# Two decoder layers with product-key experts on one core: the gather ring is cut from eight rows to five after its first 128 slots, and the rows set free hold input weights of the second layer

## The chip, the cores and the metric

One core of one Trainium2 chip runs the whole kernel as one program. The metric is the device time of one execution in microseconds (us); the median over the runs is compared. The engines are named as in the profile: PE (TensorE) multiplies matrices, PEld is its weight load, DVE is VectorE, ACT is ScalarE, POOL is GpSimd, SP is SyncE, which here only issues transfers.

## What is computed

Two layers over 256 tokens of 1024 float32 numbers. Layer 0 mixes tokens by differential attention, layer 1 by a short gated convolution; after each comes a product-key expert layer (16384 experts, 8 heads, 16 chosen each). What matters here, cut from the reference:

```python
def short_conv(h, w_in, conv_w, w_out):                     # layer 1
    bcx = h @ w_in                                          # 1024 x 3072: six chunks of 512 columns
    b_gate, c_gate, xin = bcx[..., :D], bcx[..., D:2*D], bcx[..., 2*D:]
    ...
    return (b_gate * zc) @ w_out

def peer_ffn(h, w_q, sub_keys, u_tab, v_tab):               # after both layers
    q = (xt @ w_q).reshape(T, PEER_HEADS, 2, PEER_HALF)
    ...                                                     # top 16 of 16 x 16 pairs, for each of 8 heads
    act = jnp.einsum('chkd,cd->chk', u_tab[ib], xb)         # each token reads its own 128 rows of u
    act = (jax.nn.gelu(act.astype(F32)) * gb).astype(xb.dtype)
    return jnp.einsum('chk,chkd->cd', act, v_tab[ib])       # and its own 128 rows of v
```

## The kernel before

The 256 tokens of each layer are two halves of 128, and a half of a layer is a *window*: windows 0 and 1 are layer 0, windows 2 and 3 are layer 1. Each window has 128 *slots* (8 heads by 16 experts), 512 in all (`ALL`). In slot s every one of the 128 tokens gathers one expert, the row u and the row v together: 8 KB on each of 128 partitions, 1 MiB a slot. The slots are counted in the order of their issue.

The gathered rows go round a ring in memory, `ring`, of eight rows (`RING = 8`, `ring_at`, `slot`). What one slot does:

- POOL waits until `v_used` says that slot s - 8 has been read, and issues the gather of slot s (L737).
- DVE waits for the landing and takes the dot product with the token (L1421), in `dot`.
- ACT makes gelu, weight and a diagonal matrix of it (L960, L962, L966), in `weigh`.
- PE adds diagonal times v to the sum in two banks (L634, in `add_expert`) and raises `v_used`.

PE reads the slot's row last, so from landing to that matmul the row is occupied, and a new request for it can go out only then.

Beside the slots run *sides*: generators that hang the rest of the work (the mixing, projections, ranking) on slot numbers. `AT` gives for window n the offset at which each step begins, counted from the start of window n - 1; window 2 is prepared in slots 128 to 255, window 3 in slots 256 to 383, and slots 384 to 511 have only the last rankings beside them. A projection is eight steps of one slot each (`project`), so on PE an expert's two matmuls and one projection matmul take turns.

A projection's weights are a *chunk*: 1024 rows by 512 columns, 2 MiB, written `(n, what, c)`: window, matrix (`in`, `out`, `wq`), chunk. SP issues the chunks in the order of the list `loads` (`load_stream`, L687, for the buffer `stream`, place 0, in two halves of 1 MiB that are refilled as each has been read; L703 for the places that hold a whole chunk). Since SP works in order, a load waits for all that stand before it. Windows 2 and 3 use the same matrices. The set `SHARED` names those chunks of window 1 and 3 that are still held from the window before and are not loaded again: of layer 1 these are input chunks 2 and 3, both output chunks and query chunks 2 and 3.

Of the kernel before, what the change touches and what calls it, by code (L numbers as in the profile page):

```python
# [18 lines left out]
KT = D // P  # L19
# [8 lines left out]
SLOTS = PH * TOPK  # L28
RING = 8
# [28 lines left out]
def steady_of(n):  # L58
# [27 lines left out]
          (3, "in", 2), (3, "in", 3), (3, "out", 0), (3, "out", 1), (3, "wq", 2), (3, "wq", 3)}  # L86
# [56 lines left out]
def build(nc, consts, x_rows, x_cols, bias_rows, ffn_rows, w_qkv, w_o, conv_w_in, conv_w_out, peer_w_q, peer_keys, peer_uv, out):  # L143
    with ExitStack() as ctx:
# [95 lines left out]
        w_in = {place: sem(f"w_in{place}") for place in range(2, 10)}  # L240
# [43 lines left out]
        STREAM = 0  # L284
        places = {STREAM: stream[:, :], 6: spare[:, :], 7: kept[:, 0, :], 8: kept[:, 1, :], 9: kept_work}
# [6 lines left out]
        loads += [(2, "in", 2, 6), (2, "out", 0, 8), (2, "in", 4, STREAM), (2, "in", 3, 7), (2, "out", 1, 9), (2, "in", 5, STREAM), (2, "in", 0, STREAM),  # L292
                  (2, "in", 1, STREAM), (2, "wq", 0, STREAM), (2, "wq", 1, STREAM)]
        loads += [(3, "in", 4, STREAM), (2, "wq", 2, 6), (3, "in", 5, STREAM), (2, "wq", 3, 7), (3, "in", 0, STREAM), (3, "in", 1, STREAM),
                  (3, "wq", 0, STREAM), (3, "wq", 1, STREAM)]
        held_at = {}
        for place in places:
            for i, load in enumerate(load for load in loads if load[3] == place):
                held_at[load[:3]] = place, i

        def ring_at(s):
            return (2, 3, 6, 7, 4, 5, 0, 1)[s % RING]

        def slot(s):

            return ring[:, ring_at(s), :], uv_in[ring_at(s)], 16 * (s // RING + 1)
# [25 lines left out]
        def weights(n, what, c):  # L332

            place, before = held(n, what, c)
            return places[place].rearrange("p (k n) -> p k n", k=KT)
# [14 lines left out]
        def _(pe):  # L350
# [7 lines left out]
            def wait_weights(n, what, c, k):  # L358

                place, before = held(n, what, c)  # L360
                if place == STREAM:
                    if k % DEEP == 0:
                        pe.wait_ge(part_in[k // DEEP], 16 * (before + 1))
# [8 lines left out]
            def project_part(pool, n, what, c, src, ks, columns=slice(0, CHUNK), part=""):  # L372

                by_row = weights(n, what, c)
# [5 lines left out]
                for k in ks:  # L380
                    wait_weights(n, what, c, k)
                    mm = nc.tensor.matmul(bank[:, 0:width], src[:, k, :], by_row[:, k, columns], start=(k == 0), stop=(k == KT - 1))  # L382
                    if k == KT - 1:
                        mm.then_inc(pool.written_sem(key), 1)
                    elif k % DEEP == DEEP - 1 and held(n, what, c)[0] == STREAM:
                        mm.then_inc(part_used, 1)
# [72 lines left out]
            def front():  # L459
# [6 lines left out]
                by_row = weights(0, "in", 0)  # L466
                bank = take(pp, (0, "in", 0))
                for k in every:
# [7 lines left out]
                    mm = nc.tensor.matmul(bank[:, :], xT[:, k, :], by_row[:, k, :], start=(k == 0), stop=(k == KT - 1))  # L476
# [178 lines left out]
        def _(sp):  # L655
# [23 lines left out]
            def load_stream(n, what, c, before, previous):  # L679

                size = DEEP * CHUNK
                for part in range(PARTS):
                    if previous is not None and part < PARTS - 1:
                        sp.wait_ge(part_used, (PARTS - 1) * (before - 1) + part + 1)
                    elif previous is not None:
                        written(sp, pp, last_reader(*previous))
                    sp.dma_start(stream[:, part * size:(part + 1) * size],  # L687
                                 matrix_of(n, what, c)[:, part * size:(part + 1) * size]).then_inc(part_in[part], 16)
# [3 lines left out]
            for n, what, c, place in loads:  # L692
                if place == STREAM:
                    load_stream(n, what, c, held(n, what, c)[1], previous.get(place))
                elif (n, what, c) not in ((0, "in", 0), (0, "in", 2)):
# [7 lines left out]
                    sp.dma_start(places[place], matrix_of(n, what, c)).then_inc(w_in[place], 16)  # L703
# [9 lines left out]
        def _(pool):  # L713
            for n in range(WINDOWS):
                for k in range(SLOTS):
# [16 lines left out]
                    else:  # L732
                        pool.wait_ge(v_used, s - RING + 1)
# [748 lines left out]
```

## Time and profile before

| what | value |
|---|---|
| median of 3 runs | 1538.14 us (1537.93 to 1538.52) |
| span of the profiled execution | 1536.8 us |
| PE, DVE, ACT, POOL busy in it | 88%, 65%, 39%, 38% |
| moved by DMA | 623.93 MB, of which 536.90 MB by the gathers' queue q0 and 78.91 MB by SP's queue q1 |
| TensorE clock granted over the span | 0.988 |

The profile comes from an execution of its own; its span counts from the first to the last instruction, and the median time is 1.3 us longer. The span of 1536.8 us is the profiled execution's own time, since no other is given for it. MB are millions of bytes, KB in the rows of transfers are 1024 bytes. A transfer's "landing" is counted from the start of the instruction that issues it. A row of the timeline has start, duration, engine, line, operation, tiles, and in square brackets how long the engine had been idle and what ended that.

### The profile page before, as it was taken

How to read it: one execution, taken by the hardware profiler on the slowest of the kernel's cores; microseconds unless marked ns; L12 is line 12 of the kernel's file. 1: busy time of each engine (PE TensorE's matmuls, PEld its weight loads, DVE VectorE, ACT ScalarE, POOL GpSimd, SP SyncE). 2: the span in 40 equal slices, each digit the busy share in tenths (PEclk: the TensorE clock that was granted, in tenths of full speed). 3: DMA queues.
4: the chain of work that ended last, by engine and by line, in shares of the span. 5: the costliest groups of instructions: out<-in, count | busy, mean ns of one | idle time of the engine just before them, and what ended most of it. 6: DMA issues, size and time to landing. Idle time of an engine off the chain costs nothing.

```text
span 1536.8 us, 12644 instructions
## 1 busy us (share of the span) xinstructions
PE 1348.4 (88%) x3294; PEld 571.0 (37%) x3294; DVE 1004.6 (65%) x2483; ACT 596.0 (39%) x1805; POOL 577.8 (38%) x518
## 2 busy tenths in 40 slices
PE   8999899899877999889887889898989789778787
PEld 3453343344323433334332334343434333222222
DVE  5777877786566876446478636666657867765454
ACT  1334363643333433334334424243434344343333
POOL 0033333344313333335544434343434444334442
PEclk9999999999999999999999999999999999999999
DMA  9669999999999999999999999999999999999996
GB/s 389 260 249 420 420 423 420 414 393 421 422 423 423 422 420 421 421 421 421 422 421 412 421 422 418 422 415 420 407 421 420 419 412 419 420 414 410 422 422 277
DMA packets 85896, 623.93 MB, mean 406 GB/s; under 512 B 9536, under 2 KB 9664, under 8 KB 12480
## 3 DMA queue, kind: packets, MB, share of 16 engines
q0 software_dynamic: 74016, 536.90, 84.5%
q1 hardware_dynamic: 10080, 78.91, 12.4%
q10 hardware_dynamic: 1728, 7.31, 1.2%
q8 instruction: 26, 0.43, 0.1%
q14 instruction: 46, 0.38, 0.1%
HBM read 622.04 MB, written 1.05 MB: 405 GB/s over the span
## 4 chain that ended last, share of the span: by engine, by line
DMA 51%; PE 28%; DVE 11%; ACT 6%; issue 3%; SPq 0%; POOL 0%; DVEq 0%; POOLq 0%
DMA ring<-in_peer_uv_dram,idx 50%; PE acc L634 19%; PE pp L382 7%; DVE ring L1421 6%; DMA ring<-in_w_qkv_dram 2%; ACT diag L966 1%; ACT weight L962 1%; ACT L960 1%; ACT gelu L960 1%; ACT L823 1%; PE tt L397 1%; ACT work L786 1%; DVE top_i L1138 0%; PE ss L456 0%; DVE mx L1077 0%
## 5 line engine op out<-in xcount | busy, mean ns | idle before, releaser
L634 PE MATMUL acc<-ring,diag 128*128 128x512 f32 x2048 | 995.8, 612 | 172.4 <-ACT diag L966 168.6
L1421 DVE CUSTOM_DVE_ANT_0 ring<-ring,xf 128x1024 f32<-128x1024 f32 x512 | 627.4, 1226 | 465.9 <-DMA ring<-in_peer_uv_dram,idx 456.9
L737 POOL DMA_INDIRECT ring<-in_peer_uv_dram,idx x510 | 572.8, 1123 | 936.8 <-PE acc L634 828.5
L634 PEld LDWEIGHTS acc<-ring,diag 128*128 128x128 f32 x2048 | 370.4, 192 | 736.4 <-ACT diag L966 395.6
L960 ACT ACTIVATE gelu<-dots 128x1 f32<-128x1 f32 x512 | 103.7, 202 | 818.0 <-DVE dots L1421 817.7
L966 ACT ACTIVATE diag<-const,weight 128x128 f32<-128x128 f32 x512 | 205.4, 401 | 16.8
L962 ACT ACTIVATE weight<-gelu,gates 128x1 f32<-128x1 f32 x512 | 150.8, 295 | 16.6
L382 PE MATMUL pp<-stream,xT 128*128 128x512 f32 x160 | 81.5, 599 | 0.0
L382 PE MATMUL pp<-stream,rows 128*128 128x512 f32 x128 | 65.8, 596 | 0.0
L382 PEld LDWEIGHTS pp<-stream,xT 128*128 128x128 f32 x160 | 30.1, 192 | 35.6 <-issue 35.6
L1421 DVE DVE_READ_ACCUMULATOR2_ANT dots<- 128x1 f32 x512 | 42.1, 82 | 0.0
L382 PE MATMUL pp<-kept,xT 128*128 128x512 f32 x80 | 40.1, 592 | 0.0
L382 PEld LDWEIGHTS pp<-stream,rows 128*128 128x128 f32 x128 | 24.4, 192 | 30.2 <-issue 30.2
L1138 DVE FIND_INDEX8 top_i<-top,score 128x8 uint32<-128x128 f32 x128 | 34.2, 285 | 0.0
L382 PE MATMUL pp<-kept,qTa 128*128 128x512 f32 x64 | 32.2, 596 | 0.0
L382 PE MATMUL pp<-ring,xT 128*128 128x512 f32 (+1 forms) x80 | 29.3, 513 | 1.6 <-DMA ring<-in_w_qkv_dram 1.3
L1134 DVE MAX8 top<-score 128x8 f32<-128x128 f32 x128 | 28.0, 280 | 2.8 <-ACT score L819 2.5
L960 ACT ACT_TABLE_LOAD x21 | 26.9, 1283 | 0.4
L1138 DVE FIND_INDEX8 pos<-best,pick 128x8 uint32<-128x256 f32 (+1 forms) x64 | 25.9, 416 | 0.0
L382 PE MATMUL pp<-stream,xf 128*128 128x512 f32 x48 | 24.5, 592 | 0.0
L1134 DVE MAX8 best<-pick 128x8 f32<-128x256 f32 (+1 forms) x64 | 24.0, 413 | 0.4 <-DVE h L1413 0.2
L382 PEld LDWEIGHTS pp<-kept,xT 128*128 128x128 f32 x80 | 14.7, 190 | 16.3 <-issue 16.3
(153 smaller groups left out, 744.4 us busy)
## 6 DMA issues: line engine op xcount, KB each, us to landing
stream<-in_peer_w_q_dram SPq DMA_DIRECT2D x18, 1024.0 KB, 9.3
stream<-in_conv_w_in_dram SPq DMA_DIRECT2D x16, 1024.0 KB, 9.6
stream<-in_w_qkv_dram SPq DMA_DIRECT2D x8, 1024.0 KB, 10.0
ring<-in_peer_uv_dram,idx POOLq DMA_INDIRECT x510, 15.3
ring<-in_w_qkv_dram SPq DMA_DIRECT2D x2, 2048.0 KB, 26.8
stream<-in_w_o_dram SPq DMA_DIRECT2D x4, 1024.0 KB, 18.9
kept<-in_peer_w_q_dram SPq DMA_DIRECT2D x2, 2048.0 KB, 11.4
ring<-in_w_qkv_dram SPq DMA_DIRECT2D x2, 1024.0 KB, 11.8
```

The lines of the kernel that those rows point to most:

```text
L382: mm = nc.tensor.matmul(bank[:, 0:width], src[:, k, :], by_row[:, k, columns], start=(k == 0), stop=(k == KT - 1))
L397: t = nc.tensor.transpose(bank[:, j * P:(j + 1) * P], tile, ident)
L634: mm = nc.tensor.matmul(acc[half][:, :], diag[:, s % RING, :], row[:, D + half * 512:D + (half + 1) * 512], start=(k == 0), stop=(k == SLO ...
L737: nc.gpsimd.indirect_dma_start(dst, None, uv_dram, bass.IndirectOffsetOnAxis(idx[:, at:at + 1], 0)).then_inc(landed, 16)
L786: nc.scalar.activation(ex[:, i, at:at + nk], ex[:, i, at:at + nk], ACT.Exp, bias=mx[:, c, i:i + 1], accum_out=sums[:, c, i:i + 1]).then_in ...
L823: nc.scalar.activation(best_e[:, js[0]:js[-1] + 1, :], best_e[:, js[0]:js[-1] + 1, :], ACT.Exp).then_inc(best_exp, len(js))
L960: nc.scalar.activation(gelu[:, r:r + 1], dots[:, r:r + 1], ACT.Gelu_apprx_tanh).then_inc(gelu_done, 1)
L962: nc.scalar.activation(weight[:, r:r + 1], gelu[:, r:r + 1], ACT.Copy, scale=gates[:, at:at + 1]).then_inc(weight_ready, 1)
L966: nc.scalar.activation(diag[:, r, :], ident, ACT.Copy, scale=weight[:, r:r + 1]).then_inc(diag_ready, 1)
L1134: ins = nc.vector.max(t, v)
L1138: ins = nc.vector.max_index(i, t, v)
L1421: nc.vector.tensor_tensor_reduce(row[:, 0:D], row[:, 0:D], xf[:, s // SLOTS % 2, :], 1.0, 0.0, ALU.mult, ALU.add, dots[:, s % RING:s % RIN ...
```

## The change

From slot 128 on the ring has five rows, 2, 3, 4, 0, 1 (`LATER_ROWS`); for slots 0 to 127 it has the eight that it had. Slot s then waits for the last slot that used its row (`row_before`), which from slot 133 on is slot s - 5. Rows 6 and 7 become place 10, which holds the whole input chunk 5, and row 5 becomes place 11, which holds the first half (k = 0 to 3) of input chunk 0. Both are loaded once, for window 2, and window 3 uses them again: chunk (3, in, 5) joins `SHARED`, and of (3, in, 0) only the second half is loaded, into `stream` (`SECOND_HALF`). `stream` is now counted in half chunks (`stream_pieces`, `stream_at`), since pieces no longer come in pairs.

```diff
 SHARED = {(1, "in", 0), (1, "in", 4), (1, "in", 5), (1, "out", 0), (1, "wq", 3),
-          (3, "in", 2), (3, "in", 3), (3, "out", 0), (3, "out", 1), (3, "wq", 2), (3, "wq", 3)}
+          (3, "in", 2), (3, "in", 3), (3, "in", 5), (3, "out", 0), (3, "out", 1), (3, "wq", 2), (3, "wq", 3)}
...
-        places = {STREAM: stream[:, :], 6: spare[:, :], 7: kept[:, 0, :], 8: kept[:, 1, :], 9: kept_work}
+        places = {STREAM: stream[:, :], 6: spare[:, :], 7: kept[:, 0, :], 8: kept[:, 1, :], 9: kept_work,
+                  10: ring[:, 6:8, :].rearrange("p r d -> p (r d)"), 11: ring[:, 5, :]}
...
-        loads += [(2, "in", 2, 6), (2, "out", 0, 8), (2, "in", 4, STREAM), (2, "in", 3, 7), (2, "out", 1, 9), (2, "in", 5, STREAM), (2, "in", 0, STREAM),
+        loads += [(2, "in", 2, 6), (2, "out", 0, 8), (2, "in", 4, STREAM), (2, "in", 3, 7), (2, "out", 1, 9), (2, "in", 5, 10), (2, "in", 0, 11), (2, "in", 0, SECOND_HALF),
                   (2, "in", 1, STREAM), (2, "wq", 0, STREAM), (2, "wq", 1, STREAM)]
-        loads += [(3, "in", 4, STREAM), (2, "wq", 2, 6), (3, "in", 5, STREAM), (2, "wq", 3, 7), (3, "in", 0, STREAM), (3, "in", 1, STREAM),
+        loads += [(3, "in", 4, STREAM), (2, "wq", 2, 6), (2, "wq", 3, 7), (3, "in", 0, SECOND_HALF), (3, "in", 1, STREAM),
                   (3, "wq", 0, STREAM), (3, "wq", 1, STREAM)]
...
+        held_at[3, "in", 0] = held_at[2, "in", 0]
+
+        FIRST_ROWS, LATER_ROWS = (2, 3, 6, 7, 4, 5, 0, 1), (2, 3, 4, 0, 1)
+        row_of = [FIRST_ROWS[s % RING] if s < SLOTS else LATER_ROWS[(s - SLOTS) % len(LATER_ROWS)] for s in range(ALL)]
+        row_before = [max((r for r in range(s) if row_of[r] == row_of[s]), default=None) for s in range(ALL)]
+        row_count = [row_of[:s + 1].count(row_of[s]) for s in range(ALL)]
...
-            return ring[:, ring_at(s), :], uv_in[ring_at(s)], 16 * (s // RING + 1)
+            return ring[:, row_of[s], :], uv_in[row_of[s]], 16 * row_count[s]
...
+                    elif place in (10, 11):
+                        sp.wait_ge(v_used, max(s for s in range(ALL) if row_of[s] in ((6, 7) if place == 10 else (5,))) + 1)
...
-                        pool.wait_ge(v_used, s - RING + 1)
+                        pool.wait_ge(v_used, row_before[s] + 1)
```

The order of the instructions on PE, DVE, ACT and POOL stays as it was. SP's issues change at two places. The first is the preparation of window 2. Before, all of input chunks 5, 0 and 1 go through `stream` (each row is half a chunk, in the order 5, 0, 1; what a row waits for stands in brackets):

```order
L703 DMA kept<-in_conv_w_in_dram 128x4096 [waits pp_written0]
L703 DMA work<-in_conv_w_out_dram 128x4096 [waits y_ready]
L687 DMA stream<-in_conv_w_in_dram 128x2048 [waits part_used]
L687 DMA stream<-in_conv_w_in_dram 128x2048 [waits pp_written0]
L687 DMA stream<-in_conv_w_in_dram 128x2048 [waits part_used]
L687 DMA stream<-in_conv_w_in_dram 128x2048 [waits pp_written0]
L687 DMA stream<-in_conv_w_in_dram 128x2048 [waits part_used]
L687 DMA stream<-in_conv_w_in_dram 128x2048 [waits pp_written1]
```

and now chunk 5 and half of chunk 0 go to `ring` as soon as the last slots that use those rows are read:

```order
L732 DMA kept<-in_conv_w_in_dram 128x4096 [waits pp_written0]
L732 DMA work<-in_conv_w_out_dram 128x4096 [waits y_ready]
L732 DMA ring<-in_conv_w_in_dram 128x4096 [waits v_used]
L732 DMA ring<-in_conv_w_in_dram 128x2048 [waits v_used]
L714 DMA stream<-in_conv_w_in_dram 128x2048 [waits part_used]
L714 DMA stream<-in_conv_w_in_dram 128x2048 [waits pp_written0]
L714 DMA stream<-in_conv_w_in_dram 128x2048 [waits pp_written1]
```

The bytes of this place are the same; three of its six half chunks moved ahead, to the end of slot 126. The second place is the preparation of window 3. Before, on SP, from input chunk 4 to input chunk 1:

```order
L687 DMA stream<-in_conv_w_in_dram 128x2048 [waits part_used]
L687 DMA stream<-in_conv_w_in_dram 128x2048 [waits pp_written0]
L703 DMA spare<-in_peer_w_q_dram 128x4096 [waits pp_written1]
L687 DMA stream<-in_conv_w_in_dram 128x2048 [waits part_used]
L687 DMA stream<-in_conv_w_in_dram 128x2048 [waits pp_written0]
L703 DMA kept<-in_peer_w_q_dram 128x4096 [waits pp_written0]
L687 DMA stream<-in_conv_w_in_dram 128x2048 [waits part_used]
L687 DMA stream<-in_conv_w_in_dram 128x2048 [waits pp_written1]
L687 DMA stream<-in_conv_w_in_dram 128x2048 [waits part_used]
L687 DMA stream<-in_conv_w_in_dram 128x2048 [waits pp_written1]
```

and now:

```order
L714 DMA stream<-in_conv_w_in_dram 128x2048 [waits part_used]
L714 DMA stream<-in_conv_w_in_dram 128x2048 [waits pp_written0]
L732 DMA spare<-in_peer_w_q_dram 128x4096 [waits pp_written1]
L732 DMA kept<-in_peer_w_q_dram 128x4096 [waits pp_written0]
L714 DMA stream<-in_conv_w_in_dram 128x2048 [waits part_used]
L714 DMA stream<-in_conv_w_in_dram 128x2048 [waits pp_written0]
L714 DMA stream<-in_conv_w_in_dram 128x2048 [waits pp_written1]
```

Three rows of half a chunk are gone, both halves of chunk 5 and the first of chunk 0; behind the chunk into `kept` the next two pieces can follow at once, since the half of `stream` that each fills has long been read.

## Rows read from the trace of the kernel before

**Rows 1.** The page: DMA share and rate in 40 slices; queues

```profile
DMA  9669999999999999999999999999999999999996
GB/s 389 260 249 420 420 423 420 414 393 421 422 423 423 422 420 421 421 421 421 422 421 412 421 422 418 422 415 420 407 421 420 419 412 419 420 414 410 422 422 277
...
q1 hardware_dynamic: 10080, 78.91, 12.4%
```

**Rows 2.** Waits of the whole trace: total us, times, longest

```profile
DVE ring L1421 <- DMA ring<-in_peer_uv_dram,idx: 456.9, 396, 6.5
```

**Rows 3.** Busy time by stretch (columns in the first row)

```profile
core 0: us, PE busy (x) PEld busy (x) DVE busy (x) ACT busy (x) POOL busy (x), PEclk, DMA share, GB/s
904.30:966.80 62.50, 59.29 (x150) 26.64 (x149) 37.00 (x93) 23.27 (x74) 26.07 (x22) 1.00 1.01 420
979.60:1037.70 58.10, 55.49 (x140) 24.90 (x141) 39.50 (x103) 23.48 (x68) 22.48 (x20) 1.00 1.01 418
1400.00:1500.00 100.00, 79.90 (x162) 27.40 (x163) 49.66 (x81) 35.93 (x120) 42.38 (x41) 1.00 1.01 417
```

**Rows 4.** The dot products (L1421) between 1396 and 1500 us

```profile
L1421 DVE CUSTOM_DVE_ANT_0 ring<-ring,xf x43: 1224/1225/1227, 1395.3 to 1499.7; 128x1024 f32<-128x1024 f32 x43
```

**Rows 5.** Transfers by issuing line, KB each, median us to landing

```profile
stream<-in_conv_w_in_dram SPq DMA_DIRECT2D x16, 1024.0 KB, 9.6
ring<-in_peer_uv_dram,idx POOLq DMA_INDIRECT x510, 15.3
```

**Rows 6.** Timeline of one slot with nothing beside it, slots 384 and on

```profile
1469.83 1.23 DVE L1421 CUSTOM_DVE_ANT_0 ring<-ring,xf 128x1024 f32<-128x1024 f32 x1 [1.24 <-DMA ring<-in_peer_uv_dram,idx]
...
1472.12 1.98 PE L634 MATMUL acc<-ring,diag 128*128 128x512 f32 x4 [0.49 <-ACT diag L966]
...
1474.37 0.94 POOL L737 DMA_INDIRECT ring<-in_peer_uv_dram,idx  x1 [1.54 <-PE acc L634]
```

**Rows 7.** Line L737 from 92 to 93.5 us: the gather of slot 0

```profile
DMA to landing us min/median/max: 5.9/5.9/5.9
```

**Rows 8.** Line L737, whole trace: duration ns (min/median/max), first and last start

```profile
L737 POOL DMA_INDIRECT ring<-in_peer_uv_dram,idx x510: 932/937/1981, 92.3 to 1509.2; - x170
```

**Rows 9.** Timeline, slot 304's dot and release, slot 315's dot

```profile
993.01 1.23 DVE L1421 CUSTOM_DVE_ANT_0 ring<-ring,xf 128x1024 f32<-128x1024 f32 x1 [2.06 <-DMA ring<-in_peer_uv_dram,idx]
...
997.55 0.95 POOL L737 DMA_INDIRECT ring<-in_peer_uv_dram,idx  x1 [4.28 <-PE acc L634]
...
1020.34 1.22 DVE L1421 CUSTOM_DVE_ANT_0 ring<-ring,xf 128x1024 f32<-128x1024 f32 x1 [1.26 <-DMA ring<-in_peer_uv_dram,idx]
```

**Rows 10.** POOL's timeline, three issues between 1002 and 1029 us

```profile
1002.73 0.94 POOL L737 DMA_INDIRECT ring<-in_peer_uv_dram,idx  x1 [1.64 <-PE acc L634]
1005.30 0.94 POOL L737 DMA_INDIRECT ring<-in_peer_uv_dram,idx  x1 [1.64 <-PE acc L634]
...
1028.18 1.76 POOL L737 DMA_INDIRECT ring<-in_peer_uv_dram,idx  x1 [1.15 <-PE acc L634]
```

**Rows 11.** Timeline: dot and release, slots 163, 272, 280, 295 (two rows each)

```profile
591.99 1.23 DVE L1421 CUSTOM_DVE_ANT_0 ring<-ring,xf 128x1024 f32<-128x1024 f32 x1
...
597.78 1.22 POOL L737 DMA_INDIRECT ring<-in_peer_uv_dram,idx  x1 [1.63 <-PE acc L634]
...
895.78 1.22 DVE L1421 CUSTOM_DVE_ANT_0 ring<-ring,xf 128x1024 f32<-128x1024 f32 x1 [6.50 <-DMA ring<-in_peer_uv_dram,idx]
...
902.07 0.94 POOL L737 DMA_INDIRECT ring<-in_peer_uv_dram,idx  x1 [6.88 <-PE acc L634]
...
922.52 1.22 DVE L1421 CUSTOM_DVE_ANT_0 ring<-ring,xf 128x1024 f32<-128x1024 f32 x1 [2.47 <-DMA ring<-in_peer_uv_dram,idx]
...
927.57 1.96 POOL L737 DMA_INDIRECT ring<-in_peer_uv_dram,idx  x1 [3.01 <-PE acc L634]
...
959.90 1.23 DVE L1421 CUSTOM_DVE_ANT_0 ring<-ring,xf 128x1024 f32<-128x1024 f32 x1 [0.46 <-DMA ring<-in_peer_uv_dram,idx]
...
967.02 0.94 POOL L737 DMA_INDIRECT ring<-in_peer_uv_dram,idx  x1 [0.86 <-PE acc L634]
```

More of the change, by code:

```diff
@@ L239, in build @@
         keys_in = sem("keys_in")
-        w_in = {place: sem(f"w_in{place}") for place in range(2, 10)}
+        w_in = {place: sem(f"w_in{place}") for place in range(2, 12)}
         w_first_in = [sem(f"w_first_in{i}") for i in range(4)]
@@ L299, in build @@
                 held_at[load[:3]] = place, i
+        held_at[3, "in", 0] = held_at[2, "in", 0]
[3 more added lines that the diff above has]
+        row_count = [row_of[:s + 1].count(row_of[s]) for s in range(ALL)]
+        stream_pieces = []
+        for n, what, c, place in loads:
+            if place in (STREAM, SECOND_HALF):
+                stream_pieces += [(n, what, c, half) for half in range(PARTS) if half or place == STREAM]
+        stream_at = {piece: i for i, piece in enumerate(stream_pieces)}
         def ring_at(s):
-            return (2, 3, 6, 7, 4, 5, 0, 1)[s % RING]
+            return row_of[s]
         def slot(s):
-            return ring[:, ring_at(s), :], uv_in[ring_at(s)], 16 * (s // RING + 1)
+            return ring[:, row_of[s], :], uv_in[row_of[s]], 16 * row_count[s]
         def in_order(n):
@@ L330, in held, with weights @@
             return held_at[(n - 1 if (n, what, c) in SHARED else n, what, c)]
-        def weights(n, what, c):
+        def weights(n, what, c, k):
+            half, i = divmod(k, DEEP)
+            if (n, what, c, half) in stream_at:
+                i += stream_at[n, what, c, half] % 2 * DEEP
+                return stream[:, i * CHUNK:(i + 1) * CHUNK]
             place, before = held(n, what, c)
-            return places[place].rearrange("p (k n) -> p k n", k=KT)
+            if place in scattered:
+                return scattered[place][k]
+            return places[place][:, k * CHUNK:(k + 1) * CHUNK]
         def copied(eng, pool, *keys):
@@ L465, in front @@
                 pe.wait_ge(x_scaled, 1)
-                by_row = weights(0, "in", 0)
                 bank = take(pp, (0, "in", 0))
@@ L677, in load_first, with load_stream @@
                 sp.dma_start(place[:, 4 * CHUNK:], columns[:, 4 * CHUNK:]).then_inc(w_in[5], 16)
-            def load_stream(n, what, c, before, previous):
+            def load_stream(n, what, c):
                 size = DEEP * CHUNK
[L682 to L688, printed above, removed]
+                for half in range(PARTS):
+                    at = stream_at.get((n, what, c, half))
+                    if at is None:
+                        continue
+                    if at >= 2:
+                        before = stream_pieces[at - 2]
+                        if before[3] == 0:
+                            sp.wait_ge(part_used, sum(piece[3] == 0 for piece in stream_pieces[:at - 1]))
+                        else:
+                            written(sp, pp, last_reader(*before[0:3]))
+                    sp.dma_start(stream[:, at % 2 * size:(at % 2 + 1) * size],
+                                 matrix_of(n, what, c)[:, half * size:(half + 1) * size]).then_inc(part_in[at % 2], 16)
             load_first()
```

24 lines of the change are left out of this document (14 added, 10 removed).

## The prediction

> **What bounds the kernel now.** I read the page first, its line of DMA shares and rates. From the fourth to the thirty-ninth of 40 slices the transfer engines are nearly full, at 420 to 423 GB/s where nothing disturbs them [rows 1]. PE, at 88%, is close behind, so the question is which of the two stands still for the other. The waits answer it: 396 of the 512 dot products begin when their gather lands, and wait 456.9 us for it in all [rows 2]. Busy time by stretch then shows the DMA share at 1.01 in the last stage, where PE is busy for 80 of 100 us, and also at 1.01 in two stretches of window 3's preparation, where PE is busy for 59.3 of 62.5 and 55.5 of 58.1 us [rows 3]. So the transfers bound the time nearly everywhere, but in the stretches with projections by little.
>
> The price of a transferred MiB follows from the dot products of the last stage, which run at the pace of landings: from 1395.3 to 1499.7 us there are 42 steps, (1499.7 - 1395.3) / 42 = 2.486 us a slot of 1 MiB [rows 4]. I call this the pace.
>
> A gather needs 15.3 us in the median to land [rows 5], six times the pace. That is a queue and not a latency: the gather of slot 0, which had no other gather ahead, landed 5.9 us after its issue began [rows 7].
>
> **Term 1, the bytes taken away.** Three pieces of 1 MiB of window 3 are not loaded: both halves of input chunk 5 and the first half of chunk 0 (the second place in SP's order). They are of the kind of the stream rows, 1024 KB each [rows 5]. With the transfer engines full throughout the stage [rows 3], each gives back its pace: 3 x 2.486 = 7.46 us. Bytes of window 2 are the same and only move ahead, behind the loads of chunk 3 and the output chunk; they add to a burst at slots 127 to 137 in which gathers and loads share the engines. That costs nothing as long as the engines are full, and the chunks are read from offsets 30 and 38, over 20 slots (50 us) later. The other engines keep their orders and durations: cost 0. On SP the second query chunk into `kept` is followed at once by two stream pieces; nothing that was issued before them is now issued after, so no weight arrives later by much. If one did, its projection would stop PE, and every later slot with it; the shortest distance (issue at offset 62, use at 66, four slots or 10 us, against 9.6 us to landing [rows 5]) is as short before.
>
> **Term 2, the shorter ring.** Let *hold* be the time from the landing of a slot to the issue of the request that reuses its row. In a slot with nothing beside it, the dot begins at 1469.83, PE's group for it ends at 1474.10, and POOL issues at 1474.37: the hold is 4.54 us [rows 6]. With R rows at the pace a row comes round every R x 2.486 us: 19.9 us for eight, 12.43 us for five. What the hold leaves is what the request has to land in: 19.9 - 4.5 = 15.4 us, which is the median above, and 12.43 - 4.54 = 7.9 us with five. The transfer engines go empty when less is left than a request needs. That need, N, is not in the trace for an engine that is still busy with the request before, so it is bounded:
>
> - from above by the lone gather, N = 5.9 us [rows 7], since all of its start and end lie open;
> - from below by POOL's instruction and the pace, 0.94 + 2.49 = 3.4 us [rows 8, 4].
>
> I take 5.2 us, nearer to the lone gather, since it is the same operation, and only its last part can lie under the next request's start. So the engines run dry when a hold exceeds 12.43 - 5.2 = 7.2 us (6.5 us with N = 5.9; 9.0 us with N = 3.4), and what is beyond is lost.
>
> The calm slots are far from that. Holds grow where PE is slower than the pace. With a projection in each slot POOL's issues are 2.57 us apart (1002.73 to 1005.30 [rows 10]): 0.09 us more than a landing. Groups of transposes add some tenths of a us each, once. A stream piece that lands lets PE catch up, since for 2.49 us no slot comes. The three worst stretches, with their rows:
>
> - Slots 304 to 319. Slot 304 has a hold of 997.55 - 993.01 = 4.54 us [rows 9]; slot 315, with its dot at 1020.34, is released at 1028.18: 7.84 us [rows 9, 10]. That is 3.3 us in 11 slots with no load landing, 1.0 us of it by the 0.09 us and the rest by transposes. Now the piece that landed before slot 316 is gone, and the next lands by slot 320: 7.84 + 4 x 0.09 = 8.2 us.
> - Slots 273 to 295. Slot 272 had 902.07 - 895.78 = 6.29, slot 280 927.57 - 922.52 = 5.05, slot 295 967.02 - 959.90 = 7.12 us [rows 11]. The fall of 1.2 us from 272 to 280 came from the two halves of chunk 5, now gone: 7.12 + 1.2 = 8.3 us.
> - Slots 152 to 175 (window 2). Slot 163 has 597.78 - 591.99 = 5.8 us [rows 11]; the halves of chunks 0 and 1 that followed are now in memory already. Until the next landing 12 slots at 0.09 us make 1.1 us, and I estimate 0.6 us for transposes: 7.5 us.
>
> Over the 7.2 us that is 1.0 + 1.1 + 0.3 = 2.4 us, and I add an estimated 0.4 us for rankings, where the dots come late on DVE (slots 240 to 245): 2.8 us lost. With N = 5.9 it is 1.7 + 1.8 + 1.0 for the stretches, and by estimate 1.1 for rankings and 0.5 for smaller places, 6.1 us; with N = 3.4 nothing.
>
> **The sum.** The profiled span of 1536.8 us loses 7.46 and gains 2.8: 1532.1 us. The runs' median lies 1.3 us above the span, so 1538.1 - 7.5 + 2.8 = 1533.4 us. With the bounds of N it is 1530.7 and 1536.7 us.
>
> **Two rules beside the rows.** POOL's instruction lasts 0.94 us in the median and up to 1.98 us [rows 8]. With eight rows the longer ones are covered by the queue; with five they take from the 7.9 us. The Trainium skill (SBUF — State Buffer, section Who interferes with whom) says that a DVE instruction in a two-port mode locks GpSimd out for its whole length, so that a gather's descriptors come late while DVE works. By that rule N would be 1 us longer wherever DVE is busy; that would be the second case below, since N = 5.9 is nearly that. The trace shows the longer instructions but not what made them so. The skill (DMA: Bandwidth & Descriptors, section Anatomy of one DMA — SWDGE (gpsimd) path) also gives about 2.0 us of fixed cost beside the bytes; as an estimate N would then be 4.5 us, the limit 7.9 us, the loss 0.7 us and the time 1531.4 us. The lone gather's 5.9 us does not agree with it, and I stay with the row.
>
> **The rivals.**
>
> *The ring gives back most of the gain (25%).* N is 5.9 us or a little more in the stretches with projections. For it: the 5.9 us was measured; two stretches exceed the limit even in the lower case. Against it: while other transfers are under way the start of a request lies under them. Time: 1536.7 us, up to 1538.5 us if the smaller peaks count double.
>
> *Five rows are too few throughout (17%), and the kernel is slower.* The place is slots 133 to 383. The holds shown lie between 4.5 and 7.8 us [rows 9, 11]; I estimate their mean at 5.3 us. From N = 12.43 - 5.3 = 7.1 us on every slot there comes late, by (N - 7.1) / 5 us. With N = 7.7 this is 0.12 us for each of 250 slots, 30 us; but loads that share the engines cover about half of the slots, so about +15 us: 1546 us. At N = 7.3 it is +5 us, 1542 us with the losses at the peaks. For it: the rows show no gather that lands in under 7.9 us but the lone one [rows 5, 7]. Against it: what they show has its own queue in front, 15.3 us of it being what eight rows leave.
>
> *The transfers were hidden, or the weights arrive late (5%).* If PE bounded window 3's preparation, fewer bytes would give nothing: 1538 us. Against it stands the DMA share of 1.01 in just these stretches [rows 3].
>
> **How the numbers follow.** The forecast's case has 53%: 1533.4 us, its own range 1530.7 to 1535.5 us. This kernel's measurement tells 0.2% (3.1 us) from no change; the forecast is 0.3% faster. Faster by over 0.2% (under 1535.1 us): nearly all of the first case and a little of the second, 0.53. Within 0.2%: most of the second and the last case, 0.29. Slower: the third, 0.18. For 8 in 10 the range reaches from 1530.3 us, no loss, to 1540.5 us, which leaves out the worse part of the third case.
>
> **What the new profile would show.** If term 1 is right, q1 carries 3.15 MB less, 75.8 MB for 78.91 [rows 1]. If the account of the ring is right, gathers of the last stage land in about 7.9 us where it was 15.3, and the last stage is no longer than before. If the losses are where I put them, the GB/s of the slices at slots 152 to 175 and 273 to 320 fall by 1 to 4%, and DVE's waits there end with a gather that was issued when PE released its row less than 6 us before. I am wrong if the last stage alone grows (N above 7.9 us), or if gaps of landings appear in slots whose hold is under 6 us; and also if nothing at all is lost, since then N is near its lower bound.

## The result, and the profile after

The changed kernel takes 1572.25 us (median of 5 runs, 1569.89 to 1574.88) where the kernel before took 1538.5 us on the same chip (5 runs, 1537.93 to 1539.72). The ratio is 1.022, with an interval of 1.0208 to 1.0232: slower by 34 us. I had forecast 1533.4 us. One of the executions of the kernel before that ran beside the experiments took 4827 us, for a reason that isn't known, and is in no ratio.

The page of the changed kernel, its transfer share and rate in 40 slices (the rows that answer to [rows 1]):

```profile
DMA  9669999999999999999999999999999999999998
GB/s 391 245 274 421 420 424 418 413 405 421 422 423 423 379 406 371 421 407 393 400 403 383 394 419 391 414 385 413 392 401 396 398 393 392 408 399 409 414 418 336
...
q1 hardware_dynamic: 9504, 75.76, 11.7%
```

The last row shows the bytes: 75.76 MB on SP's queue, 3.15 MB less, as forecast. The slices show where the time went. Up to the twelfth or thirteenth slice, which is the first 128 slots with all eight rows, they read as before. From there to the last but one nearly all are below the 420 GB/s of [rows 1], at 371 to 421, and not only in the three stretches that I had named. The share says nine tenths or more in all these slices, so it does not show the loss; the rate does.

The waits of the whole trace, and the gathers (L766) issued between 1400 and 1500 us with their time from issue to landing:

```profile
DVE ring L1450 <- DMA ring<-in_peer_uv_dram,idx: 485.8, 399, 5.0
```

```profile
L766 POOL DMA_INDIRECT ring<-in_peer_uv_dram,idx x39: 936/937/1969, 1399.9 to 1497.4; - x39
...
DMA to landing us min/median/max: 7.3/7.9/9.3
```

DVE waits 28.9 us more for landings than in [rows 2]. A gather lands in 7.9 us in the median, as forecast: a row comes round every 5 x 2.486 = 12.43 us, 4.54 us of it are the hold. But this stage is longer too, which I had excluded. From 1399.0 to 1497.8 us the changed kernel has 40 dot products, so a step is 98.8 / 39 = 2.533 us, where [rows 4] gave 2.486.

Busy time of two stretches, one in window 3's preparation and one in the last stage:

```profile
core 0: us, PE busy (x) PEld busy (x) DVE busy (x) ACT busy (x) POOL busy (x), PEclk, DMA share, GB/s
800.00:900.00 100.00, 77.62 (x181) 30.43 (x180) 68.78 (x164) 40.98 (x124) 39.46 (x37) 1.00 0.99 390
1400.00:1500.00 100.00, 77.36 (x156) 26.41 (x156) 48.30 (x80) 35.91 (x120) 39.69 (x39) 1.00 1.01 414
```

No compute engine took over as the bound: PE is at 78% and 77%, at a granted clock of 1.00. In the last stage 39 gathers were issued in 100 us where [rows 3] has 41 on POOL.

I worked out the time between the landing of one slot and of another for whole stages from the trace. Each number is a difference of two landings, in us:

| slots | before | changed | five rows only | six rows only | six rows, chunk 5 kept |
|---|---|---|---|---|---|
| 0 to 128 | 386.2 | 385.2 | 387.1 | 385.7 | 385.8 |
| 128 to 256 | 366.3 | 382.2 | 377.4 | 366.9 | 366.4 |
| 256 to 384 | 358.9 | 365.6 | 370.6 | 358.9 | 354.2 |
| 384 to 508 | 312.4 | 322.3 | 320.2 | 312.6 | 312.7 |

The last three columns are of experiments below. The changed kernel loses 15.9 us in the second stage, 9.9 us in the last, and in the third 6.7 us after what the bytes saved. With 7.5 us for the bytes the third stage lost 14.2 us, and the ring as a whole 40 us, where I had reckoned 2.8. Each column is one execution, and kernels with five rows differ by 5 to 13 us from one execution to the next, so their columns show where the time goes, and medians what it costs.

### The profile page after: what moved, and what is told of

Its sections match the earlier page's. It is cut to its first block, busy times and chain, and to the rows that moved or that the text cites. A ratio compares the mean times of both kernels' runs of the same rounds, so it can differ in the third digit from the quotient of the medians.

```text
span 1568.0 us, 12640 instructions
## 1 busy us (share of the span) xinstructions
PE 1359.1 (87%) x3294; PEld 573.4 (37%) x3294; DVE 1004.9 (64%) x2483; ACT 596.2 (38%) x1805; POOL 570.8 (36%) x518
## 3 DMA queue, kind: packets, MB, share of 16 engines
q1 hardware_dynamic: 9504, 75.76, 11.7%
## 4 chain that ended last, share of the span: by engine, by line
DMA 41%; PE 34%; DVE 13%; ACT 7%; issue 4%; SPq 0%; POOL 0%; DVEq 0%; POOLq 0%
DMA ring<-in_peer_uv_dram,idx 40%; PE acc L656 23%; PE pp L405 9%; DVE ring L1450 7%; ACT diag L995 2%; DMA ring<-in_w_qkv_dram 2%; ACT weight L991 1%; ACT gelu L989 1%; ACT L989 1%; ACT L852 1%; PE tt L420 1%; ACT work L815 1%; PE ss L479 0%; DVE top_i L1167 0%; DVE mx L1106 0%
## 5 line engine op out<-in xcount | busy, mean ns | idle before, releaser
L766 POOL DMA_INDIRECT ring<-in_peer_uv_dram,idx x510 | 566.6, 1111 | 981.8 <-PE acc L656 876.7
L405 PE MATMUL pp<-stream,rows 128*128 128x512 f32 x80 | 40.9, 592 | 0.0
L405 PE MATMUL pp<-ring,rows 128*128 128x512 f32 x48 | 24.7, 596 | 0.0
L479 PEld LDWEIGHTS ss<-keysT,qT 128*128 128x128 f32 x128 | 18.7, 209 | 10.4 <-issue 10.4
## 6 DMA issues: line engine op xcount, KB each, us to landing
ring<-in_w_qkv_dram SPq DMA_DIRECT2D x2, 1024.0 KB, 11.7
```

The source lines that it names most:

```text
L405: mm = nc.tensor.matmul(bank[:, 0:width], src[:, k, :], weights(n, what, c, k)[:, columns], start=(k == 0), stop=(k == KT - 1))
L479: mm = nc.tensor.matmul(bank[:, j * P:(j + 1) * P], qT[:, j, :], keysT[:, 4 * c + j, :], start=True, stop=True)
L766: nc.gpsimd.indirect_dma_start(dst, None, uv_dram, bass.IndirectOffsetOnAxis(idx[:, at:at + 1], 0)).then_inc(landed, 16)
```

## The experiments

I had these theories. **A**: requests come too late; a gather needs more than I took for it while the engines are also busy with another, and five rows leave too little. **B**: the 16 transfer engines run unevenly, and a deep ring lets the quick ones go ahead; each row less takes a little of that. **C**: the three pieces loaded early, or their new place in SP's order, cost the time. **D**, formed after the two runs with a later request: DVE's dot product holds up POOL's issue.

### One part of the change at a time

Each of these kernels is an edit of the changed kernel, and of each only the lines that matter are shown. The first keeps the five rows from slot 128, and loads everything as the kernel before does, in window 2 too:

```diff
-        loads += [(3, "in", 4, STREAM), (2, "wq", 2, 6), (2, "wq", 3, 7), (3, "in", 0, SECOND_HALF), (3, "in", 1, STREAM),
+        loads += [(3, "in", 4, STREAM), (2, "wq", 2, 6), (3, "in", 5, STREAM), (2, "wq", 3, 7), (3, "in", 0, STREAM), (3, "in", 1, STREAM),
...
-        held_at[3, "in", 0] = held_at[2, "in", 0]
```

> Five rows from slot 128 on, but every weight loaded as before, so no byte is saved and no load moves. Theory A (late requests: a gather asked for while the transfer engines are busy needs about 7.4 us to land, so with five rows every hold over 12.4 - 7.4 = 5.0 us empties them) and theory B (uneven engines: eight rows let the sixteen transfer engines run apart, so that a pause of one costs nothing) both put the whole loss in the ring: the time of the changed kernel plus the 7.5 us of bytes, 1577 to 1582 us. Theory C (the ring is innocent, the moved loads and their burst at slot 127 cost the time): 1538 to 1542 us.

Measured: 1576.29 us (4 runs, 1570.49 to 1583.11), ratio 1.0258 [1.0227, 1.0289]. The rows alone cost 38 us, as much as the changed kernel loses beside what the bytes give back: with 6.7 to 7.5 us for these it would take 1579 to 1580 us, within the four runs here. C falls here as the cause; a part of a few us would be hidden by the scatter.

The second has eight rows throughout and window 2's loads as before, and does not load window 3's three half chunks. Its projections with input chunk 5 and with the first half of chunk 0 read another matrix that is in memory, so its output isn't the layer's:

```diff
-        held_at[3, "in", 0] = held_at[2, "in", 0]
+        held_at[3, "in", 0] = held_at[3, "in", 5] = held_at[2, "out", 0]
...
+        row_of = [FIRST_ROWS[s % RING] for s in range(ALL)]
```

> Eight rows throughout and the loads of window 2 as before; of window 3 the three half chunks are not loaded, with SP's order of the changed kernel there, and the two projections read another chunk that lies in memory (chunk 0 of the output matrix), so that their result is not the layer's. Theories A and B: 1538.5 - 7.5 = 1531 us. Theory C, if the order of window 3's loads matters: above 1536 us.

Measured: 1531.67 us (4 runs), ratio 0.9954 [0.9936, 0.9972], which is 6.7 us less by the medians and 7.1 by the ratio. Slots 256 to 384 take 351.9 us, 7.0 less than before. The 7.46 us that term 1 gives the bytes lie within the interval. Its page shows the same bytes as the changed kernel and a rate that is nearly that of [rows 1]:

```profile
GB/s 391 261 252 421 420 421 422 420 395 421 422 423 424 420 421 422 421 421 422 421 416 409 421 420 413 422 399 422 422 420 422 416 416 417 421 416 409 423 421 274
...
q1 hardware_dynamic: 9648, 75.76, 12.0%
```

The third and fourth are the first with six and with seven rows:

```diff
-        FIRST_ROWS, LATER_ROWS = (2, 3, 6, 7, 4, 5, 0, 1), (2, 3, 4, 0, 1)
+        FIRST_ROWS, LATER_ROWS = (2, 3, 6, 7, 4, 5, 0, 1), (2, 3, 4, 5, 0, 1)
```

> Six rows from slot 128 on, loads as before. Theory A: holds may reach 14.9 - 7.4 = 7.5 us, which only a few slots exceed: 1540 to 1544 us. Theory B: the loss falls by degrees with the depth, 40 us at five rows, some two thirds at six: 1555 to 1565 us. Theory C: 1538.5 us.

> Seven rows from slot 128 on, loads as before. Theory A: no hold exceeds 17.4 - 7.4 = 10 us, 1538 to 1540 us. Theory B: one third of the loss stays, 1545 to 1552 us. Theory C: 1538.5 us.

Measured: 1538.62 us with six rows (10 runs), ratio 1.0002 [0.9992, 1.0011]; 1537.97 us with seven (10 runs), 1.0000 [0.9990, 1.0009]. Eight, seven and six rows take the same time, and five take 38 us more. That is an edge, where B expected a slope (1555 to 1565 us with six), so B as I had it isn't what costs the 38 us. A expected 1540 to 1544 us with six, a little too much. The engines do even out with each row: from the first to the last of a gather's 16 engines to finish, between 1250 and 1500 us, it takes 8.5 us in the median with eight rows, 5.9 with seven, 3.4 with six and 1.4 with five. A form of B in which this reserve is used up only at five rows isn't excluded by the edge. The gathers with six rows, between 1250 and 1500 us:

```profile
L765 POOL DMA_INDIRECT ring<-in_peer_uv_dram,idx x100: 932/936/1968, 1250.8 to 1498.8; - x100
...
DMA to landing us min/median/max: 9.4/10.3/11.3
```

The median is again nearly all that the ring leaves: 6 x 2.486 - 4.54 = 10.4 us.

### How long a gather needs: fewer rows in the last stage

The last stage has no projections, so its holds are nearly constant. Three kernels load as before and keep eight rows up to slot 383; from slot 384 they have five, four and three (rows `(2, 3, 4, 0, 1)`, `(2, 3, 4, 0)`, `(2, 3, 4)`):

```diff
-        row_of = [FIRST_ROWS[s % RING] if s < SLOTS else LATER_ROWS[(s - SLOTS) % len(LATER_ROWS)] for s in range(ALL)]
+        row_of = [LATER_ROWS[(s - 3 * SLOTS) % len(LATER_ROWS)] if 3 * SLOTS <= s < ALL else FIRST_ROWS[s % RING] for s in range(ALL)]
```

> Eight rows up to slot 383, five from slot 384 on, where nearly nothing but the slots runs; loads as before. By the changed kernel's trace the last 124 slots lose about 10 us: theory A, from the issues that last 1 us longer and the rankings, 1545 to 1549 us. If the loss needs projections beside the slots: 1538 to 1541 us.

> Four rows from slot 384 on, so that the ring itself must set the pace: a slot takes (hold + time to land) / 4. If a gather needs the 5.9 us of the lone one: (4.54 + 5.9) / 4 = 2.61 us a slot, about +16 us in all. If it needs the 7.4 us that theory A supposes under load: 2.99 us a slot, about +63 us.

> Three rows from slot 384 on: (hold + time to land) / 3. With 5.9 us to land: 3.48 us a slot, +125 us. With 7.4 us: 3.98 us, +188 us. If the time to land falls from four rows to three, a part of it is the queue in front; if it stays, it is a latency.

Measured: 1551.94 us with five (4 runs, 1548.85 to 1557.85), ratio 1.0083 [1.0067, 1.0098], so 13 us for the calm stage alone, where I had expected 7 to 11; 1618.94 us with four and 1684.53 us with three (one run each), 80 and 146 us more, where a need of 7.4 us would have given 63 and 188. Four rows, the stretch and the gathers:

```profile
core 0: us, PE busy (x) PEld busy (x) DVE busy (x) ACT busy (x) POOL busy (x), PEclk, DMA share, GB/s
1400.00:1500.00 100.00, 66.12 (x129) 22.85 (x128) 40.59 (x65) 28.75 (x96) 35.28 (x32) 0.97 0.90 335
```

```profile
L765 POOL DMA_INDIRECT ring<-in_peer_uv_dram,idx x32: 932/937/1921, 1400.8 to 1498.5; - x32
...
DMA to landing us min/median/max: 5.6/7.7/8.9
```

Three rows, the same two views:

```profile
1400.00:1500.00 100.00, 64.24 (x107) 22.68 (x105) 36.77 (x63) 26.16 (x81) 27.85 (x27) 0.85 0.75 273
```

```profile
L765 POOL DMA_INDIRECT ring<-in_peer_uv_dram,idx x27: 936/937/1852, 1399.4 to 1499.1; - x27
...
DMA to landing us min/median/max: 5.3/6.0/7.9
```

This is the disputed number. With four rows and 100 / 32 = 3.1 us between issues, 7.7 / 3.1 = 2.5 gathers are under way at a time; each lands in 7.7 us although the engines are idle a tenth of the time. With three rows fewer are under way (6.0 / 3.7 = 1.6), and it is 6.0 us, that of the lone gather [rows 7]. The same split is seen within one kernel. With four rows the gathers of slots 388 to 505 that had two others under way when they were issued (102) landed in 7.9 us in the median (6.0 to 9.3), those that had one (13) in 6.0. With three rows 99 had one under way and landed in 5.7 us in the median, and 12 had two and took 7.1.

The ring's arithmetic closes with it. Counted from the landing itself, which is 0.13 us before the dot's start, the hold of these slots is 4.67 us in the median; with its longer cases the mean is 4.90 us with four rows and 4.99 with three. With mean times to land of 7.71 and 5.98 us, a slot should take (4.90 + 7.71) / 4 = 3.15 and (4.99 + 5.98) / 3 = 3.66 us, and it takes 3.15 and 3.66 (390.6 and 453.8 us for slots 384 to 508).

So a gather that shares the engines with two others needs N = 7.7 us, a typical value and not a least one, and five rows leave it 7.9 us by the hold of 4.54, or 12.43 - 4.67 = 7.76 by that from the landing. The margin is 0.1 to 0.2 us, and nearly any hold beyond 4.7 us is lost time.

### The version that keeps the gain

Six rows cost nothing, so rows 6 and 7 can keep input chunk 5 for both windows; chunk 0 goes by the stream as before:

```diff
...
-        held_at[3, "in", 0] = held_at[2, "in", 0]
...
-        FIRST_ROWS, LATER_ROWS = (2, 3, 6, 7, 4, 5, 0, 1), (2, 3, 4, 0, 1)
+        FIRST_ROWS, LATER_ROWS = (2, 3, 6, 7, 4, 5, 0, 1), (2, 3, 4, 5, 0, 1)
```

> Six rows from slot 128 on, and the two rows set free hold input chunk 5 for both windows: 2 MiB less are loaded, chunk 0 is streamed as before. Theory A (a late request empties the engines; six rows ask early enough, as the run with six rows alone showed at ratio 1.0002): 1538.4 - 5.0 = 1533.4 us. Theory C (the burst of loads at slot 127 costs, of which this kernel keeps two thirds): above 1536 us.

Measured: 1533.44 us (7 runs, 1532.83 to 1534.41), ratio 0.9969 [0.9958, 0.9980], 4.95 us less than before for 2 x 2.486 = 4.97. It is faster than both kernels. Its page has 76.81 MB on SP's queue, and rates near those of before:

```profile
GB/s 390 261 243 422 420 423 420 420 395 422 421 423 423 400 416 416 422 419 414 421 420 401 421 419 404 419 419 421 413 421 422 412 416 421 412 419 419 417 421 326
...
q1 hardware_dynamic: 9648, 76.81, 12.1%
```

### Six rows, but the request as late as with five

If the moment of the request counts and not the number of rows, then six rows with five rows' request must be slow as well. From slot 133 on, POOL also waits until the slot five back has been read. The sister waits only for the first half of that slot's additions, some 0.9 us earlier:

```diff
+                        if s >= SLOTS + 5:
+                            pool.wait_ge(v_used, s - 4)
```

```diff
+                    elif half == 0:
+                        mm.then_inc(half_used, 1)
...
+                        if s >= SLOTS + 5:
+                            pool.wait_ge(half_used, s - 4)
```

> Six rows from slot 128 on, loads as before, but POOL also waits for the slot five back to be read before it asks, as it must with five rows. Theory A (what counts is how early a gather is asked for): as the run with five rows alone, 1570 to 1583 us. If the memory rows themselves or their places mattered: 1538.6 us, as six rows alone.

> As the run before, but POOL waits only for the first half of the additions of the slot five back, which end about 0.9 us before the second. In a calm slot a gather then has about 8.8 us to land where six rows give 10.4 and five 7.9. By the runs with four and three rows a gather needs about 7.7 us while the engines serve another: holds may grow by 1.1 us before the engines run dry. Theory A: a loss of a quarter to a half of the five-row kernel's 38 us, 1546 to 1558 us. If the lone 5.9 us counted, 1539 to 1541 us.

Measured: 1610.63 us (4 runs), ratio 1.0472 [1.0454, 1.0489], far beyond what I expected; and for the earlier request 1559.77 us (4 runs), ratio 1.0150 [1.0126, 1.0173], just above the most I expected (1558). The first miss has two parts. One is the added wait, which makes the issue itself later: from PE's release to the start of POOL's instruction it is 0.27 us in the kernel before and 0.78 us with the full request. The other is D, below. By the median hold of the calm stage the runs fall in order:

| kernel | rows | hold, us | against before, us |
|---|---|---|---|
| six rows, one wait | 6 | 2.2 | 0 |
| six rows, half request | 6 | 4.22 | +21 |
| five rows, loads as before | 5 | 4.67 | +38 |
| six rows, full request | 6 | 5.17 | +72 |

The hold is counted here from the landing of the slot five back to the issue, as the median over slots 390 to 505. Six rows are as slow as five, and slower, once they ask as late: so the moment of the request decides, and the number of rows only through it. That is A. By A alone the last step of the table, 0.5 us of hold, should cost 0.5 / 5 = 0.1 us in each of some 376 slots, 38 us. It cost 34, but that the two agree is luck: by the two traces 25 of it fall on slots 384 to 508, 0.2 us in each, and only 13 on the 256 slots before.

So A alone doesn't explain these issues, nor the uneven ones of the changed kernel. The timeline of the kernel with the full request, DVE and POOL:

```profile
1480.59 1.23 DVE L1451 CUSTOM_DVE_ANT_0 ring<-ring,xf 128x1024 f32<-128x1024 f32 x1 [1.26 <-DMA ring<-in_peer_uv_dram,idx]
1480.65 1.98 POOL L767 DMA_INDIRECT ring<-in_peer_uv_dram,idx  x1 [3.00 <-PE acc L655]
...
1483.07 1.23 DVE L1451 CUSTOM_DVE_ANT_0 ring<-ring,xf 128x1024 f32<-128x1024 f32 x1 [1.25 <-DMA ring<-in_peer_uv_dram,idx]
1483.14 1.97 POOL L767 DMA_INDIRECT ring<-in_peer_uv_dram,idx  x1 [0.51 <-issue]
```

Both times POOL's instruction starts 0.06 or 0.07 us after a dot and takes 1.98 us in place of 0.94. In the fourteen traces of this case 1662 issues start x = 0.06 to 1.0 us after the start of such a dot, and every one takes 0.94 + (1.10 - x) us to within 0.02 us: POOL comes to the end of its 0.94 us only then, as if it had begun 0.12 us before the dot's end. An issue that starts less than 0.05 us after the dot isn't held. In the calm slot of [rows 6] the issue starts 1474.37 - 1469.83 = 4.54 us after its slot's dot, which is 4.54 - 2.49 = 2.05 us after the next dot's start and 0.43 us before the third's. A request that is 0.43 us late, or a little more, meets that dot and loses up to 1 us more. That was theory D.

### The dot product replaced by a sum

From slot 128 on the dot is a plain sum of the gathered row: one operand, no product written, and as long (1.22 us). The result isn't the layer's. Once with five rows, once with six and the full request:

```diff
-                nc.vector.tensor_tensor_reduce(row[:, 0:D], row[:, 0:D], xf[:, s // SLOTS % 2, :], 1.0, 0.0, ALU.mult, ALU.add,
-                                               dots[:, s % RING:s % RING + 1]).then_inc(dot_done, 1)
+                if s < SLOTS:
...
+                else:
+                    nc.vector.tensor_reduce(dots[:, s % RING:s % RING + 1], row[:, 0:D], AX.X, ALU.add).then_inc(dot_done, 1)
```

> Five rows from slot 128 on, loads as before, and from slot 128 on the dot product, which reads two operands from memory, is replaced by a plain sum over the row, which reads one and takes about the same time (the result is then not the layer's; the work of the other engines is the same). The traces so far suggest theory D: a gather issued x us after a dot began lasts about 0.94 + (1.05 - x) us, as if the dot held POOL until it ends. Theory D: every issue lasts 0.94 us, and a good part of the 38 us of five rows goes, 1545 to 1562 us. If the long issues have another cause: they stay, 1570 to 1583 us.

> Six rows, asked for as with five and 0.5 us late by the second wait, which took 1610.6 us with the dot product; here with the plain sum instead, as in the run before. Theory D: with dots the 0.5 us put the issue just behind the start of the next dot, which cost another 1 us; with sums that is gone: 1565 to 1585 us. If the long issues have another cause: 1600 to 1612 us.

Measured: 1561.16 us (4 runs), ratio 1.0146 [1.0129, 1.0163], 15 us less than with the dot; and 1574.86 us (4 runs), ratio 1.0230 [1.0205, 1.0256], 36 us less. Both are within what D expected. With the full request and the sum, POOL starts 0.07 us after DVE and is not held:

```profile
1440.49 1.22 DVE L1455 TENSOR_REDUCE dots<-ring 128x1 f32<-128x1024 f32 x1 [1.25 <-DMA ring<-in_peer_uv_dram,idx]
1440.56 0.94 POOL L767 DMA_INDIRECT ring<-in_peer_uv_dram,idx  x1 [1.55 <-PE acc L655]
```

So D is shown: the dot holds POOL's instruction, and of the 38 us of five rows some 15 are by it (with the scatter of the five rows' runs, 10 to 20). From slot 133 on, the trace with five rows has 105 issues that last over 1 us, 64 us beyond 0.94 in all; with the sum 10 are left. It also tells what was mixed into the 34 us above: with the sum in both kernels, the 0.5 us of hold costs 1574.86 - 1561.16 = 13.7 us and not 34, and in slots 384 to 508 10.8 us, which is A's 0.1 us a slot.

The sum differs in two things, an operand fewer and no product written. These two runs don't tell which of them frees POOL, but other instructions of DVE do, already in the kernel before. The ring and most tiles lie in SBUF, the core's large memory, and `acc`, the banks that PE sums in, in PSUM. A TENSOR_TENSOR of 512 columns with one input in SBUF (`h`) and one in PSUM (`acc`) writes its whole result and doesn't hold the issue; one with both inputs in SBUF (`pos_f` and `const`) does:

```profile
486.37 0.69 DVE L1413 TENSOR_TENSOR h<-h,acc 128x512 f32<-128x512 f32 x1 [0.58 <-PE acc L634]
486.60 0.94 POOL L737 DMA_INDIRECT ring<-in_peer_uv_dram,idx  x1 [1.26 <-PE acc L634]
...
161.68 1.22 DVE L1177 TENSOR_TENSOR pick<-pos_f,const 128x1024 f32<-128x1024 f32 x1
162.36 1.36 POOL L737 DMA_INDIRECT ring<-in_peer_uv_dram,idx  x1 [2.50 <-PE acc L634]
```

Of the issues in the fourteen traces that start under a TENSOR_TENSOR (0.05 us or more after it began, 0.25 us or more before it ends), all 191 were held where both of its inputs lay in SBUF, and none of 67 where one lay in PSUM. So it is the second input from SBUF, and not the product written. The Trainium skill (SBUF — State Buffer, section Who interferes with whom) says that a DVE instruction with two inputs in SBUF takes the second through an interface that it shares with GpSimd and so contends with a GpSimd instruction that reads SBUF, and that a tensor_reduce never does. By that rule the dot holds the gather's issue, which takes its indices from `idx` in SBUF, and the sum doesn't: the trace agrees, 1.98 against 0.94 us. The page also infers that making descriptors would not be held by such an instruction with two inputs; here the measurement differs, 191 issues of 191, and it decides. In the prediction I had quoted the page's two-port modes, which is not what these rows show. Another 22 us stay with no dot in the way: by the starts on DVE, the trace with five rows and the sum is 10.8 us longer than the one before in slots 128 to 256, 8.3 us in slots 256 to 384 and 3.1 us in slots 384 to 508. So 19 of the 22 us lie where projections lengthen the holds.

## Why the prediction was wrong

**Term 1 was right.** Three MiB were forecast at 7.46 us and gave 6.7 to 7.1 in the run with the bytes alone, and two gave 4.95 for 4.97. That transfers bound the time throughout held as well. That pieces loaded early cost nothing held for the two of chunk 5, with six rows; for all three with five rows the scatter leaves it open.

**The step that failed is "I take 5.2 us", with its bound "from above by the lone gather, N = 5.9 us".** N is 7.7 us. I had argued that a request whose start lies under another's transfer needs less than one alone, since part of it is hidden. The runs show the opposite: alone or with one other under way 5.7 to 6.1 us, with two others 7.7 to 7.9. A lone gather is therefore no bound from above. What holds a request back while others are under way isn't shown; the 16 engines have its predecessors' packets to move first, which would do it. The trace before had a hint of that on another queue: by its packets, a load of 1 MiB on SP's queue (issued at 69.24 us) moved its first one 0.97 us after its issue with the engines idle and landed after 5.0 us; with them busy the first one moved some 3.45 us after the issue, and the median landing is 9.6 us [rows 5].

**From that the limit on the hold fell** from my 7.2 us to 12.43 - 7.7 = 4.7 us. The three stretches I had picked out by holds of 7.5 to 8.3 us were no special places: of the holds of slots 140 to 383, some seven in ten are above 4.7 us in the trace before, with a mean of 5.4 us (I had estimated 5.3), and the calm hold of 4.54 us [rows 6] is just below it. I had defined the hold from the landing and read it from the dot's start, 0.13 us later, which alone would have moved the limit little.

**The third rival named the mechanism and mis-sized it.** At N = 7.7 it reckoned 30 us for slots 133 to 383, and halved that to 15 for the loads that share the engines. The changed kernel lost 15.9 + 14.2 = 30.1 us there and the one with five rows alone 11.1 + 11.7 = 22.8, so the halving took off too much; that the full 30 us was met is partly luck, since the dot's part was not in it. It also left out the last stage, where 0.2 us of margin would have to absorb every disturbance; it does not, and 9.9 us were lost. In the landings of the changed kernel's slots 384 to 508 the gaps beyond the pace add up to 14.5 us, where the kernel before has 4.6. Some 9 us of the 14.5 stand at gathers issued over 5.0 us after the landing five slots back. The rest is at gathers issued in time; there, some packets of 8 KB take 0.6 to 1.3 us in place of 0.31, twice beside the stores of window 2's output, and what lengthens them I don't know. One place of the first kind in the changed kernel, POOL and DVE:

```profile
1351.48 1.22 DVE L1450 CUSTOM_DVE_ANT_0 ring<-ring,xf 128x1024 f32<-128x1024 f32 x1 [0.47 <-DMA ring<-in_peer_uv_dram,idx]
1351.56 1.96 POOL L766 DMA_INDIRECT ring<-in_peer_uv_dram,idx  x1 [2.04 <-PE acc L656]
...
1356.45 1.22 DVE L1450 CUSTOM_DVE_ANT_0 ring<-ring,xf 128x1024 f32<-128x1024 f32 x1 [0.42 <-DMA ring<-in_peer_uv_dram,idx]
...
1359.60 1.23 DVE L1450 CUSTOM_DVE_ANT_0 ring<-ring,xf 128x1024 f32<-128x1024 f32 x1 [1.25 <-DMA ring<-in_peer_uv_dram,idx]
```

The request at 1351.56 starts 0.08 us after a dot, takes 1.96 us, and lands for the dot at 1359.60, 3.15 us after the dot before it: 0.66 us lost by this one slot. With eight rows the same long instruction [rows 11, at 927.57] had 15 us of queue in front of it.

**POOL's long instructions were weighed too lightly.** I had noted their 1.98 us [rows 8] and that the trace didn't show what made them so. It did: nearly all of them start under a dot, or under another instruction of DVE with two inputs in SBUF. I had put the lock at N = 5.9, as the case of 25%; it comes on top of 7.7, and cost some 15 us.

**Of my own signs of being wrong** one came true as written: gaps of landings in slots whose hold is under 6 us. The other, that the last stage alone grows with N above 7.9 us, didn't: all three stages grew, and N at 7.7 with the disturbances was enough. That the last stage would be no longer than before was wrong too.

What stays open: of the five rows' 38 us, some 15 are by the dot. The other 22 us are only placed, 19 of them in the stages with projections; the long holds there aren't separated from slow packets that find no reserve in the ring (what is left of B). With five rows and the dot the runs of a kernel scatter by 5 to 13 us, where the kernel before stays within 1 to 3. With five rows and the sum they lie within 2.3 us, so the dot seems to have a part in the scatter; with the later request and the sum they scatter by 8.6 again, and this was not tested further.

## What to carry to other kernels

The depth of a ring of transfers is the hold plus the time a request needs *with the engines occupied*, over the pace; here (4.5 + 7.7) / 2.486 = 4.9, so five rows sit on the edge and six are safe. Count the hold with its longer cases and not by its calm one. Measure that time by taking rows away until the pace breaks, in the calmest stage, and not by a request that had the engines to itself. Before memory is taken from a ring, try one row fewer at a time: most of the gain here (5 of 7.5 us) was to be had with two rows, and the third turned it into a loss of 34. Where gathers are asked for just in time, also look at what DVE runs at the moment of the issue.

## What the runs showed of the hardware

- A gather of 1 MiB lands 5.7 to 6.1 us after its issue begins, in the median, when at most one other is under way, and after 7.9 us (6.0 to 9.3) when two are (four rows; with three rows 7.1).
- DVE's fused multiply and sum over 128 x 1024 f32 holds up a gather's issue on POOL until 0.12 us before its own end: 0.94 us become up to 1.98. So does a TENSOR_TENSOR with both inputs in SBUF (191 issues of 191). A plain sum of the same length doesn't, nor does a TENSOR_TENSOR with one input in PSUM (none of 67).
- A second semaphore wait ahead of POOL's issue, the one that ends last, made it 0.51 us later (0.78 for 0.27 us).
- The time is flat from eight to six rows, to within 0.1%, and then +2.6% with five.
- Between 1250 and 1500 us the last of the 16 transfer engines finished a gather 8.5 us after the first with eight rows, by their semaphore updates; with six 3.4 us, with five 1.4 to 1.8 us. Evening out to 3.4 us cost nothing, as six rows show.
